# A two-block transformer on one core: attention steps placed by quarters of a unit, weights' high part ahead of chunk steps, first stage reordered

## The chip, the cores and the metric

One NeuronCore of a Trainium2 chip runs the whole program. The metric is device time in microseconds (us) of one execution; lower is better. TensorE is called PE, VectorE DVE, ScalarE ACT, GpSimd POOL, and SP is the queue that issues the weights' transfers.

## The reference

512 tokens of width 1024 go through two blocks of two layers each. A layer of the first block is a gated feed-forward part, a mixer and a second feed-forward part, each behind a root-mean-square norm. The mixer is what the change is about:

```python
h = rms_norm(x, gn[2])
hq, hf, hi, hg, aq, ak, av, gate_a, gate_b = jnp.split(h @ w_in[l], IN_SPLITS, axis=-1)
y_hg = hgrn2_mixer(hq, hf, hi, hg, lb_all[l], hgrn_head_gain[l]) @ w_branch_hgrn[l]
y_at = swa_sink_attention(aq, ak, av, attn_sinks[l]) @ w_branch_attn[l]
mixed = jax.nn.sigmoid(gate_a) * y_hg + jax.nn.sigmoid(gate_b) * y_at
x = x + rms_norm(mixed @ w_out[l], gn[3])
```

`swa_sink_attention` has 8 heads of 64 (2 key heads), blocks of 128 queries that see their own and the previous block of keys, a penalty by distance, and a sink in the softmax. `hgrn2_mixer` is a gated linear recurrence with 4 heads. Weights and activations are float32.

## The kernel before

**Products.** Every weight is scaled and cut into two fp16 parts, as is every activation. ACT makes the high part (`hi`, L1822), DVE the low one (`lo`, L1092), of a slot of 128 x 2048 elements; there are two slots, and SP refills one when its low part is done. A product is three fp16 matmuls (`product`, L466 to L468). A slot of weights is a unit. `hi(s)` waits for the slot's transfer and for the unit that used the slot before, `lo(s)` waits for `hi`, and PE's unit n+2 waits for `lo`, so both run while PE is at unit n+1. A full unit of 256 columns is 48 matmuls of 512 columns.

**The mixer** has 22 units in `MIX_ORDER` (`hf hq hf hi hq aq hg aq hi aq hg aq gate ak gate av` and six times `gate`), then four units of branch products (`branch_part`). Between them PE does small steps, by slots q that `SLOTS` hands to the units. Slots 0 to 22 are the chunk steps of the recurrence: `level_scores` (L664), `diag_scores` (L672), `off_scores` (L687), `head_out` (L695), `head_norm` (L481), `head_scale` (L487); a slot is a chain over the engines. POOL makes exponents (L2211) once PE's scores of a level are done, ACT takes exponentials of them (`decays`, L2000 to L2009) and the root (L1841), DVE makes decayed factors, merges scores and finishes a head (`head_post`, L1381 to L1387). Units of two slots do one of them in the middle, if they are cut in halves, and the other at the end.

**The attention** is cut into 8 items h = 2n + kv (block n, key head kv). An item has three PE steps: `attn_scores` (L722), `attn_transpose` (L732), `attn_out` (L742). In between, DVE subtracts the penalty and finds the maximum (`attn_softmax`, L1397 to L1407), ACT takes exponentials (L2035) and DVE scales them (`attn_probs`, L1419); ACT copies the transposed probabilities (L2040); of the output ACT makes the high part (L2045) and DVE the low part (`attn_low`, L1426), which frees the item's PSUM banks for item h+2. Items 0 and 1 have half the keys. Item kv of block n starts at slot 21 + 3n or 23 + 3n, its steps lie in three slots one after another (`ATTN_SLOT`, `attn_steps`), and slots 23 to 34 hold nothing else. Slots 31 to 34 lie between the first branch products.

Each engine runs its list in order. ACT's and DVE's lists come from loops over units: ACT does unit n's slots, then `hi`, then the evacuation of unit n; DVE does the slots, then waits for the evacuation and makes `lo`.

**The first stage.** PE runs 20 warming matmuls (`warm`, L1027), the bias rows (L1033), 32 warming matmuls, then four transposes of the normed x (`turned`, L503), which fill h by groups g for the first half of the tokens. `first_units` then takes units 0 and 1 in turns: `part(0, g, 0)`, `part(1, g, 0)` for g = 0 to 3. ACT issues the transfers of x blocks 2 and 3 ahead of the square sums of blocks 0 and 1. DVE makes the low weights of unit 0, splits h for groups 0 and 1, makes those of unit 1 (`lo_first`, L1099), splits groups 2 and 3 (L1140), and copies the bias rows.

## Time and profile before

| | us |
|---|---|
| three runs, median | 2728.15 (2725.31 to 2728.27) |
| the profiled execution | 2728.2 |
| its span in the trace | 2726.4 |
| PE busy | 2689.0 |
| DVE busy | 1846.8 |
| ACT busy | 1323.3 |
| POOL busy | 144.2 |

Layer 1's mixer ends with the branch and output products behind 640 us of the trace, layer 2's behind 1658. A busy PE is drawn with modelled ends: a matmul of 512 columns is drawn 0.38 us long while the next one starts 0.216 us after it. An idle time before an instruction is given in brackets with what ended it.

### The profile page before, as it was taken

How to read it: one execution, taken by the hardware profiler on the slowest of the kernel's cores; microseconds unless marked ns; L12 is line 12 of the kernel's file. 1: busy time of each engine (PE TensorE's matmuls, PEld its weight loads, DVE VectorE, ACT ScalarE, POOL GpSimd, SP SyncE). 2: the span in 40 equal slices, each digit the busy share in tenths (PEclk: the TensorE clock that was granted, in tenths of full speed). 3: DMA queues.
4: the chain of work that ended last, by engine and by line, in shares of the span. 5: the costliest groups of instructions: out<-in, count | busy, mean ns of one | idle time of the engine just before them, and what ended most of it. 6: DMA issues, size and time to landing. Idle time of an engine off the chain costs nothing.

```text
span 2726.4 us, 44390 instructions
## 1 busy us (share of the span) xinstructions
PE 2689.0 (99%) x17512; PEld 1730.8 (63%) x17512; DVE 1846.8 (68%) x2793; ACT 1323.3 (49%) x2116; POOL 144.2 (5%) x119
## 2 busy tenths in 40 slices
PE   9999999999999999999999999999999999999998
PEld 6886476644688746885476644688646555465554
DVE  6994376656799628994385656799536776457754
ACT  5663365543566425663365543566424544346442
POOL 1000022100100001000021100100000002000020
PEclk9999999999999999999999999999999999999999
DMA  5443322222333333443312222444333222321312
GB/s 166 110 121 109 116 63 70 89 78 70 109 108 108 123 101 93 122 109 116 109 62 70 90 78 85 124 116 115 120 112 101 78 83 72 111 79 62 109 62 85
DMA packets 317434, 266.18 MB, mean 98 GB/s; under 512 B 8908, under 2 KB 280524, under 8 KB 316656
## 3 DMA queue, kind: packets, MB, share of 16 engines
q1 hardware_dynamic: 314416, 254.57, 30.5%
q10 hardware_dynamic: 2272, 7.58, 1.1%
q0 software_dynamic: 608, 2.11, 0.3%
q8 instruction: 96, 1.57, 0.2%
q14 instruction: 42, 0.34, 0.0%
HBM read 257.40 MB, written 4.21 MB: 96 GB/s over the span
## 4 chain that ended last, share of the span: by engine, by line
PE 93%; DVE 4%; ACT 2%; DVEq 1%; issue 0%; DMA 0%; SPq 0%; ACTq 0%; POOL 0%
PE pu L466 14%; PE pu L467 14%; PE pu L468 14%; PE pm L466 6%; PE pm L468 6%; PE pm L467 6%; PE pu L594 6%; PE pu L592 6%; PE pu L593 6%; PE pm L592 2%; PE pm L594 2%; PE pm L593 2%; PE pm L893 2%; PE pm L664 2%; PE pm L880 1%; DVE w_lo L1092 1%
## 5 line engine op out<-in xcount | busy, mean ns | idle before, releaser
L1092 DVE SCALAR_TENSOR_TENSOR w_lo<-stage,w_hi 128x2048 f16<-128x2048 f32 (+1 forms) x156 | 353.0, 2263 | 393.0 <-ACT w_hi L1822 388.7
L1822 ACT ACTIVATE w_hi<-stage 128x2048 f16<-128x2048 f32 (+1 forms) x147 | 273.3, 1859 | 487.6 <-PE pm L468 376.9
L466 PE MATMUL pu<-h_hi,w_hi 128*128 128x512 f16 x912 | 347.6, 381 | 5.9 <-DVE w_lo L1092 5.9
L467 PE MATMUL pu<-h_lo,w_hi 128*128 128x512 f16 x912 | 347.0, 381 | 0.0
L468 PE MATMUL pu<-h_hi,w_lo 128*128 128x512 f16 x912 | 346.7, 380 | 0.0
L466 PE MATMUL pu<-w_hi,arena 128*128 128x512 f16 x512 | 194.0, 379 | 0.0
L467 PE MATMUL pu<-w_lo,arena 128*128 128x512 f16 x512 | 194.0, 379 | 0.0
L468 PE MATMUL pu<-w_hi,arena 128*128 128x512 f16 x512 | 194.0, 379 | 0.0
L466 PE MATMUL pm<-w_hi,arena 128*128 128x512 f16 x512 | 194.0, 379 | 0.0
L467 PE MATMUL pm<-w_lo,arena 128*128 128x512 f16 x512 | 194.0, 379 | 0.0
L468 PE MATMUL pm<-w_hi,arena 128*128 128x512 f16 x512 | 194.0, 379 | 0.0
L1912 ACT ACTIVATE w_hi<-stage 128x768 f16<-128x768 f32 (+1 forms) x140 | 120.1, 858 | 112.7 <-PE pu L594 112.7
L466 PEld LDWEIGHTS pu<-h_hi,w_hi 128*128 128x128 f16 x912 | 91.1, 100 | 128.8 <-issue 30.6
L468 PEld LDWEIGHTS pu<-h_hi,w_lo 128*128 128x128 f16 x912 | 89.5, 98 | 108.6 <-issue 1.7
L592 PE MATMUL pu<-arena 128*128 128x256 f16 x576 | 157.0, 273 | 0.4 <-ACT arena L1926 0.4
L594 PE MATMUL pu<-h_hi,w_lo 128*128 128x256 f16 x576 | 157.0, 273 | 0.0
L592 PE MATMUL pu<-h_hi,w_hi 128*128 128x256 f16 x576 | 157.0, 273 | 0.0
L593 PE MATMUL pu<-arena 128*128 128x256 f16 x576 | 157.0, 273 | 0.0
L593 PE MATMUL pu<-h_lo,w_hi 128*128 128x256 f16 x576 | 157.0, 273 | 0.0
L594 PE MATMUL pu<-arena 128*128 128x256 f16 x576 | 157.0, 273 | 0.0
L467 PEld LDWEIGHTS pu<-h_lo,w_hi 128*128 128x128 f16 x912 | 89.5, 98 | 95.2 <-issue 3.1
L1234 DVE SCALAR_TENSOR_TENSOR arena<-arena 128x1536 f16<-128x1536 f32 x72 | 126.3, 1754 | 0.0
(332 smaller groups left out, 6227.6 us busy)
## 6 DMA issues: line engine op xcount, KB each, us to landing
stage<-in_w_in_dram SPq DMA_DIRECT2D x136, 512.0 KB, 4.6
stage<-in_w_ffn_gate_dram SPq DMA_DIRECT2D x88, 512.0 KB, 4.0
stage<-in_w_ffn_up_dram SPq DMA_DIRECT2D x88, 512.0 KB, 5.2
stage<-in_w_ffn_down_dram SPq DMA_DIRECT2D x80, 512.0 KB, 4.0
stage<-in_w_out_dram SPq DMA_DIRECT2D x40, 512.0 KB, 4.2
stage<-in_w_in_dram SPq DMA_DIRECT2D x24, 256.0 KB, 3.2
stage<-in_w_ffn_down_dram SPq DMA_DIRECT2D x16, 256.0 KB, 4.2
stage<-in_w_branch_hgrn_dram SPq DMA_DIRECT2D x8, 512.0 KB, 3.5
```

What stands on the lines that cost most here:

```text
L466: nc.tensor.matmul(ps, w1, r_hi, start=first, stop=False)
L467: nc.tensor.matmul(ps, w1, r_lo, start=False, stop=False)
L468: return nc.tensor.matmul(ps, w2, r_hi, start=False, stop=last)
L592: nc.tensor.matmul(ps, w1, r1, start=first and k == 0, stop=False, skip_group_check=not first)
L593: nc.tensor.matmul(ps, w1, r2, start=False, stop=False, skip_group_check=not first)
L594: last = nc.tensor.matmul(ps, w2, r1, start=False, stop=k == 3, skip_group_check=not first)
L664: last = nc.tensor.matmul(pm[i % 2][:, b * P // 2:(b + 1) * P // 2].rearrange("p (n l) -> p n l", l=half), lev[:, 2 * pair + 1, b * P:(b + ...
L893: last = nc.tensor.matmul(ps[:], v_tok[:, b, hd * P:(hd + 1) * P], AT[:, b], start=b == 0, stop=b == NB - 1)
L1092: V.scalar_tensor_tensor(out=w_lo[:, s, 0:n], in0=stage[:, s, 0:n], scalar=WSCALE, in1=w_hi[:, s, 0:n], op0=ALU.mult, op1=ALU.subtract).th ...
L1234: V.scalar_tensor_tensor(out=e_lo[:, 0:1536], in0=sums[:, 4 * s + 1:4 * s + 4].rearrange("p a b -> p (a b)"), scalar=WSCALE, in1=e_hi[:, 0 ...
L1822: A.activation(w_hi[:, s, 0:n], stage[:, s, 0:n], ACT.Copy, scale=WSCALE).then_inc(hi_split, 1)
L1912: return A.activation(w_hi[:, s, first:last], stage[:, s, first:last], ACT.Copy, scale=WSCALE)
```

## The change

- The attention leaves the slots. Each unit from 16 on is done in four quarters, and `ATTN_STEPS` names for each of the three steps the quarter behind which item h has it (a quarter of a unit is 4 of 8 k for one half of the columns; the first four branch products count as quarters 23 to 26). Scores and transpose of an item are four quarters apart from item 2 on, transpose and output one.
- DVE's and ACT's orders from unit 16 on are written out, item by item, in place of the loops.
- In units 3 to 15 ACT makes the high part of the weights (`hi`) behind all but the last slot of the unit, where it did so behind all of them. DVE does the unit's evacuation and `lo` inside the last slot, ahead of `invert_head` and `head_post`.
- First stage: 12 warming matmuls between the second and the third transpose in place of 32 ahead of the first; in the first feed-forward part PE does all four groups of unit 0, then those of unit 1 (`by_unit`); DVE copies the bias rows first and makes unit 1's low weights behind all four splits of h; ACT issues x blocks 2 and 3 behind the high weights of unit 0.

The functions `attn_exp`, `attn_taken`, `attn_high` and `gate` hold what ACT's branches for the attention steps and the gates held. The diff, cut:

```diff
@@ -66,10 +66,12 @@
-SLOTS = consecutive((0, 0, 0, 1, 2, 1, 2, 1, 2, 1, 2, 1, 2, 2, 2, 2, 2, 2, 2, 1, 1, 2) + (0, 2, 0, 2))
-MIX_SLOTS, LAST_SLOTS = SLOTS[:MIX_UNITS], SLOTS[MIX_UNITS:]
+MIX_SLOTS = consecutive((0, 0, 0, 1, 2, 1, 2, 1, 2, 1, 2, 1, 2, 2, 2, 2, 2, 0, 0, 0, 0, 0))
 AHEAD = 4
-ATTN_SLOT = (21, 23)
+ATTN_UNIT = 16
+ATTN_STEPS = ((0, 3, 5, 8, 11, 14, 17, 20), (3, 6, 9, 12, 15, 18, 21, 24), (4, 7, 10, 13, 16, 19, 22, 25))
 MIX2_ORDER = [("aq", 0), ("ak", 0), ("av", 0), ("aq", 1), ("ak", 1), ("ag", 0), ("av", 1), ("ag", 1), ("cu", 0), ("cu", 1),
               ("bq", 0), ("bk", 0), ("bv", 0), ("bg", 0), ("bv", 1), ("bg", 1), ("cg", 0), ("cg", 1)]
@@ -165,14 +167,9 @@
         self.j, self.jper = 0, {}
-def attn_steps(q):
-    found = []
-    for kv in range(2):
-        n, step = divmod(q - ATTN_SLOT[kv], 3)
-        if 0 <= n < NB:
-            found.append((step, 2 * n + kv))
-    return sorted(found)
+def attn_steps(quarter):
+    return [(step, at.index(quarter)) for step, at in sorted(enumerate(ATTN_STEPS), reverse=True) if quarter in at]
...
@@ -517,9 +514,14 @@
                 pe.wait_ge(y_park, t.next("y_park", NB))
                 t.next("evac", 2)
                 pe.wait_ge(split, t.next("split"))
+                if by_unit:
+                    for g in range(4):
+                        pe.wait_ge(h_ready, base + g + 1)
+                        part(0, g, 0)
                 for g in range(4):
-                    pe.wait_ge(h_ready, base + g + 1)
-                    part(0, g, 0)
+                    if not by_unit:
+                        pe.wait_ge(h_ready, base + g + 1)
+                        part(0, g, 0)
                     if g == 0:
                         pe.wait_ge(split, t.next("split"))
                     part(1, g, 0)
...
@@ -762,7 +764,10 @@
                         diag_scores(hd)
                     if step == 4:
                         off_scores(hd)
-                for step, h in attn_steps(q):
+            def attn(quarter):
+                for step, h in attn_steps(quarter):
                     (attn_scores, attn_transpose, attn_out)[step](h)
...
                         col_half(s, 0, P).then_inc(unit_done, 1)
+                    elif n >= ATTN_UNIT:
+                        for i in range(4):
+                            last = col_half(s, i // 2, 256, range(4 * (i % 2), 4 * (i % 2) + 4))
+                            if i == 3:
+                                last.then_inc(unit_done, 1)
+                            if i % 2 and slots:
+                                mixer_slot(slots.pop(0))
+                            attn(4 * (n - ATTN_UNIT) + i - 1)
                     else:
                         col_half(s, 0, 256)
...
                         unit_ready()
                         pe.wait_ge(evac_a, first_a + MIX_ACT - 1 + n)
                         pe.wait_ge(o_ready, t.now("o_ready"))
                     branch_part(n, 0, e)
-                    for q in slots:
-                        mixer_slot(q)
+                    attn(quarter)
                 pe.wait_ge(at_ready, t.next("at_ready", 2))
                 for n in range(4):
...
@@ -1032,14 +1044,16 @@
             for e in range(2):
                 last = nc.tensor.matmul(pm[2 + e][0:A_HEADS, :], rel_tab, rel_hot[:, e * T:(e + 1) * T], start=True, stop=True)
             last.then_inc(rel_done, 1)
-            warm(32)
             pe.wait_ge(id_land, 16)
             pe.wait_ge(xn_ready, 2)
-            for g in range(4):
-                turned(set_b, xn, 0, g)
+            turned(set_b, xn, 0, 0)
+            turned(set_b, xn, 0, 1)
+            warm(12)
+            turned(set_b, xn, 0, 2)
+            turned(set_b, xn, 0, 3)
             for l in range(DEPTH):
                 with t.layers(0, PER1, 1):
-                    ffn(set_a, set_b)
+                    ffn(set_a, set_b, l == 0)
                     mixer()
                     ffn(set_a, set_b)
...
                         levels(hd * 8 + 7)
+                    if unit_work:
+                        unit_work()
                 if step == 1 and 1 <= hd <= HG_HEADS:
                     invert_head()
                 if step == 2 and 1 <= hd <= HG_HEADS:
                     head_post(hd - 1)
-                steps = attn_steps(q)
-                for step, h in steps:
-                    if step == 0:
-                        attn_softmax(h)
-                    if step == 2:
-                        attn_low(h)
-                for step, h in steps:
-                    if step == 0:
-                        attn_probs(h)
+                if unit_work and hd >= HG_HEADS:
+                    unit_work()
             def first_levels():
...
             def mixer():
-                pending = False
                 first_a = t.now("evac_a")
                 lo(1)
-                for n, (kind, part) in enumerate(MIX_ORDER):
+                def unit_work(n):
+                    kind, part = MIX_ORDER[n]
                     s = n % 2
                     banks = set_a[2 * s:2 * s + 2] if n < 2 else pu[2 * s:2 * s + 2]
                     if n == 2:
                         v.drain()
-                    if pending:
-                        v.wait_ge(evac_a, first_a + pending)
-                        pending = 0
+                    if n and evacuated(n, True) > evacuated(n - 1, True):
+                        v.wait_ge(evac_a, first_a + evacuated(n, True))
                     if n == 2:
                         first_levels()
...
                     elif kind == "aq":
                         normed(aq[:, part], banks[0][:], 0.125).then_inc(evac, 1)
-                    else:
-                        pending = evacuated(n + 1, True)
                     if n >= 2:
                         lo(s)
...
@@ -1505,12 +1512,50 @@
                             for b in range(NB):
                                 last = V.tensor_tensor_scan(hG[:, 2 * part + e, b * P:(b + 1) * P], ones[:], tb[:, e, b * P:(b + 1) * P], 0.0, ALU.mult, ALU.add)
                         last.then_inc(g_ready, 1)
-                    for q in MIX_SLOTS[n + 1] if n + 1 < MIX_UNITS else ():
+                for n in range(ATTN_UNIT):
+                    slots = list(MIX_SLOTS[n])
+                    for q in slots[:-1]:
                         mixer_slot(q)
+                    if slots:
+                        mixer_slot(slots[-1], lambda: unit_work(n))
+                    else:
+                        unit_work(n)
+                first_slot, second_slot = MIX_SLOTS[ATTN_UNIT]
+                mixer_slot(first_slot)
+                attn_softmax(0)
+                attn_probs(0)
+                mixer_slot(second_slot)
+                attn_softmax(1)
+                attn_low(0)
+                unit_work(ATTN_UNIT)
+                attn_probs(1)
+                attn_softmax(2)
+                attn_low(1)
+                unit_work(ATTN_UNIT + 1)
+                attn_probs(2)
+                attn_softmax(3)
+                attn_low(2)
+                attn_probs(3)
+                unit_work(ATTN_UNIT + 2)
+                attn_softmax(4)
+                attn_low(3)
+                attn_probs(4)
+                attn_softmax(5)
+                attn_low(4)
+                unit_work(ATTN_UNIT + 3)
+                attn_probs(5)
+                attn_softmax(6)
+                attn_low(5)
+                unit_work(ATTN_UNIT + 4)
+                attn_probs(6)
+                attn_softmax(7)
+                attn_probs(7)
+                unit_work(ATTN_UNIT + 5)
+                attn_low(6)
+                attn_low(7)
                 t.next("o_done")
                 t.next("evac_a", MIX_ACT)
-                for q in sum(LAST_SLOTS, ()):
-                    mixer_slot(q)
                 v.wait_ge(evac_a, first_a + MIX_ACT)
                 for n in range(4):
...
@@ -1781,16 +1826,14 @@
             pre(xn, 0)
             pre(xn, 1)
-            lo_first(0)
-            split_h(set_b, 0, 0, g0)
-            split_h(set_b, 0, 1, g0)
-            lo_first(1)
-            split_h(set_b, 0, 2, g0)
-            split_h(set_b, 0, 3, g0)
             v.wait_ge(rel_done, 1)
             for e in range(2):
                 last = V.tensor_copy(rel_row[:, e * T:(e + 1) * T], pm[2 + e][0:A_HEADS, :])
             last.then_inc(rel_copied, 1)
+            lo_first(0)
+            for g in range(4):
+                split_h(set_b, 0, g, g0)
+            lo_first(1)
             pre(xn, 2)
             pre(xn, 3)
...
+            def attn_exp(h):
...
+            def attn_taken(h):
...
+            def attn_high(h):
...
+            def gate(n):
...
-                for n, (kind, part) in enumerate(MIX_ORDER):
+                for n, (kind, part) in enumerate(MIX_ORDER[:ATTN_UNIT]):
                     banks = set_a[2 * (n % 2):2 * (n % 2) + 2] if n < 2 else pu[2 * (n % 2):2 * (n % 2) + 2]
                     if n == 2:
                         for p in range(AHEAD):
                             decays(p)
+                    for q in MIX_SLOTS[n][:-1]:
+                        mixer_slot(q)
                     if n < 2:
                         s_.wait_ge(unit_done, t.next("unit_done"))
                     else:
                         hi(n % 2)
+                    for q in MIX_SLOTS[n][-1:]:
+                        mixer_slot(q)
                     if kind == "ak":
...
@@ -2073,13 +2135,45 @@
                             last = A.activation(dict(hq=hq, hg=hgs)[kind][:, 2 * part + e], banks[e][:], ACT.Silu, scale=DS)
                         last.then_inc(evac_a, 1)
                     elif kind == "gate":
-                        for e in range(2):
-                            last = A.activation(gates[:, 2 * part + e], banks[e][:], ACT.Tanh, scale=0.5 * DS)
-                        last.then_inc(evac_a, 1)
-                    for q in MIX_SLOTS[n + 1] if n + 1 < MIX_UNITS else ():
-                        mixer_slot(q)
-                for q in sum(LAST_SLOTS, ()):
+                        gate(n)
+                for q in MIX_SLOTS[ATTN_UNIT]:
                     mixer_slot(q)
+                attn_exp(0)
+                hi(0)
+                gate(ATTN_UNIT)
+                attn_taken(0)
+                attn_high(0)
+                attn_exp(1)
+                attn_taken(1)
+                hi(1)
+                attn_high(1)
+                attn_exp(2)
+                gate(ATTN_UNIT + 1)
+                attn_taken(2)
+                attn_exp(3)
+                attn_high(2)
+                hi(0)
+                gate(ATTN_UNIT + 2)
+                attn_taken(3)
+                attn_high(3)
+                attn_exp(4)
+                hi(1)
+                gate(ATTN_UNIT + 3)
+                attn_taken(4)
+                attn_high(4)
+                attn_exp(5)
+                attn_taken(5)
+                hi(0)
+                attn_high(5)
+                attn_exp(6)
+                gate(ATTN_UNIT + 4)
+                attn_taken(6)
+                attn_exp(7)
+                hi(1)
+                attn_high(6)
+                gate(ATTN_UNIT + 5)
+                attn_taken(7)
+                attn_high(7)
...
@@ -2168,9 +2262,10 @@
             root(zero[:, 1:2], ones[:, 0:1], 1.0)
             for b in range(2):
                 s_.wait_ge(x_land[b], 16)
-                A.dma_start(x[:, 2 + b], x_in[:, 2 + b]).then_inc(x_land[2 + b], 16)
                 pre_sums(b)
             hi_first(0)
+            for b in range(2, NB):
+                A.dma_start(x[:, b], x_in[:, b]).then_inc(x_land[b], 16)
             s_.wait_ge(init, 2)
             split_h(set_b, 0, 0, g0)
             split_h(set_b, 0, 1, g0)
```

## Rows read from the trace of the kernel before

**Rows 1.** The page: PE's busy time, and the chain that ended last by engine.
```profile
PE 2689.0 (99%) x17512; PEld 1730.8 (63%) x17512; DVE 1846.8 (68%) x2793; ACT 1323.3 (49%) x2116; POOL 144.2 (5%) x119
...
PE 93%; DVE 4%; ACT 2%; DVEq 1%; issue 0%; DMA 0%; SPq 0%; ACTq 0%; POOL 0%
```

**Rows 2.** PE's waits, whole run: what waited, for whom, us, times, longest.
```profile
PE pm L732 <- DVE arena L1419: 7.2, 6, 1.5
PE pu L466 <- DVE w_lo L1092: 5.9, 4, 1.5
...
PE pm L742 <- ACT arena L2040: 2.3, 2, 1.2
PE pm L695 <- ACT arena L2023: 2.2, 2, 1.1
```

**Rows 3.** Stretches: length, busy by engine, clock, DMA share, GB/s.
```profile
547.12:639.80 92.68, 85.85 (x514) 45.20 (x513) 49.88 (x116) 41.92 (x105) 0.00 (x0) 0.98 0.21 69
1567.02:1658.46 91.44, 84.97 (x514) 44.44 (x513) 49.89 (x116) 41.91 (x105) 0.00 (x0) 1.00 0.21 70
639.80:650.00 10.20, 10.20 (x39) 4.27 (x40) 2.84 (x5) 1.91 (x1) 0.00 (x0) 0.81 0.00 0
1658.46:1668.66 10.20, 10.20 (x48) 4.62 (x48) 4.68 (x5) 1.91 (x1) 0.00 (x0) 1.00 0.00 0
```

**Rows 4.** PE in time order, unit 12: start, length, instruction, idle before.
```profile
483.37 0.59 PE L466 MATMUL pu<-h_hi,w_hi 128*128 128x512 f16 x1 [1.41 <-DVE w_lo L1092]
...
486.92 0.38 PE L466 MATMUL pu<-h_hi,w_hi 128*128 128x512 f16 x1
```

**Rows 5.** ACT in order of time, ahead of that wait.
```profile
474.87 0.44 ACT L2000 ACTIVATE arena<-arena 128x256 f32<-128x256 f32 x1 [6.04 <-POOL arena L2211]
...
478.97 1.90 ACT L1822 ACTIVATE w_hi<-stage 128x2048 f16<-128x2048 f32 x1
```

**Rows 6.** DVE in order of time: one item's softmax, from scores to probabilities.
```profile
560.53 1.42 DVE L1397 SCALAR_TENSOR_TENSOR arena<-cst,pm 128x256 f32<-128x256 f32 x4 [1.19 <-PE pm L722]
...
566.05 0.16 DVE L1414 TENSOR_TENSOR small<-small 128x4 f32<-128x4 f32 x1 [2.27 <-ACT small L2036]
...
566.54 1.14 DVE L1419 TENSOR_SCALAR arena<-arena,small 128x256 f32<-128x256 f32 x4
```

**Rows 7.** Groups by form, 547.12 to 639.80: count, busy us, mean ns, idle.
```profile
L2040 ACT ACTIVATE arena<-pm 128x512 f32<-128x512 f32 x12 | 6.5, 597 | 11.2 <-PE pm L732 11.2
...
L1426 DVE SCALAR_TENSOR_TENSOR arena<-pm,arena 128x256 f16<-128x256 f32 x8 | 3.4, 424 | 9.5 <-ACT arena L2045 8.9
L2045 ACT ACTIVATE arena<-pm 128x256 f16<-128x256 f32 x8 | 3.1, 383 | 23.2 <-PE pm L742 23.2
```

**Rows 8.** ACT and PE in order of time, behind unit 13: chunk step 16.
```profile
510.63 0.44 ACT L2000 ACTIVATE arena<-arena 128x256 f32<-128x256 f32 x1 [0.92 <-POOL arena L2211]
...
513.29 1.28 ACT L1841 ACT_TABLE_LOAD   x1
514.58 0.26 ACT L1841 ACTIVATE r_col<-pm,eps 128x4 f32<-128x4 f32 x1
...
515.38 0.38 PE L487 MATMUL pm<-ident,r_col 128*128 128x128 f32 x2
```

**Rows 9.** DVE and PE in order of time, around unit 10's first matmul.
```profile
455.22 2.28 DVE L1092 SCALAR_TENSOR_TENSOR w_lo<-stage,w_hi 128x2048 f16<-128x2048 f32 x1
...
457.56 0.39 PE L466 MATMUL pu<-h_hi,w_hi 128*128 128x512 f16 x1 [1.53 <-DVE w_lo L1092]
```

**Rows 10.** PE and ACT in order of time, first stage.
```profile
15.47 1.90 PE L503 MATMUL pu<-ident,arena 128*128 128x128 f32 x8 [3.13 <-DVE h_lo L1140]
16.50 1.91 ACT L1832 ACTIVATE arena<-stage 128x2048 f16<-128x2048 f32 x1 [2.74 <-DMA stage<-in_w_ffn_up_dram]
...
20.79 0.28 PE L466 MATMUL pm<-h_hi,arena 128*128 128x256 f16 x1 [1.24 <-DVE arena L1099]
```

**Rows 11.** A stretch of the first stage: PE busy, clock, DMA share, GB/s.
```profile
16.00:20.00 4.00, 3.56 (x19) 0.62 0.92 256
```

52 lines of the change are left out of this document (27 added, 25 removed).

## The prediction

> **What bounds the kernel now.** I read the page's busy shares and its chain first: TensorE (PE) is busy 2689.0 of 2726.4 us and holds 93% of the chain that ended last [rows 1]. So nothing that another engine does counts unless PE waits for it, and all there is to gain is PE's 37.4 us without work plus any stretch in which it ran at half clock. The table of waits names what ended its idle time [rows 2]: the attention's transposes waiting for the softmax on DVE (7.2 us, 6 times), first matmuls of a unit waiting for the low part of their weights (5.9 us, 4 times), the attention's output matmuls waiting for ACT (2.3), a chunk step's head matmul waiting for ACT (2.2). All of it lies in the two mixers of the first block. Two waits more, 3.13 and 1.24 us, stand at the start [rows 10]. Then I cut stretches out. The attention part of layer 1's mixer, from the end of gate unit 16 to the last attention output, takes 92.68 us with PE busy for 85.85; in layer 2 it is 91.44 and 84.97 [rows 3]. The same rows show the clock: the 10.2 us behind it hold 39 matmuls at granted clock 0.81 in layer 1 and 48 at 1.00 in layer 2. In layer 1 part of those 10.2 us ran at 1.2 GHz and not at 2.4, behind three waits that followed each other closely.
>
> **Part 1, attention by quarters.** The work is unchanged; its places change. A quarter of a unit is 12 matmuls, 12 x 0.216 = 2.59 us (0.216 is the usual step from one 512-column matmul's start to the next; the 48 in 10.2 us of layer 2's row give 0.213 [rows 3]). Before, items follow each other at unit ends, and the transpose of item h comes one unit after its scores. For a full item the chain takes, from scores to probabilities, 560.53 to 567.68 = 7.15 us: mask and maximum on DVE 3.3, exponentials on ACT 2.2, scaling 1.63 [rows 6]; a short or half unit doesn't cover it, so PE stood still.
> After, scores(h) and transpose(h) have four quarters and three other attention steps between them, about 13 us. The test is whether the written orders let the chain run in time, so I walked all 26 quarters from 547.12 on with the durations of [rows 6, 7], 1.90 for a high part [rows 5] and 2.29 for a low part [rows 9]. The pattern is the same for every item:
> - From out(h-1) to transpose(h): two quarters and a scores step (about 1.16 us) = 6.3 us. In that time the orders ask for high(h-1) 0.38, then either exponentials 2.2 and scaling 1.63, or low(h-1) 0.42, a whole weights' low part 2.29 and scaling 1.63, with some 0.3 for hand-overs: 4.5 to 5.1. Spare: 1.1 us (items 5 and 2) to 1.8 (item 4).
> - From out(h-2) to scores(h): one quarter, 2.59, against high 0.38 and low 0.42: 1.5 spare.
> - From transpose(h) to out(h): one quarter against two copies of 0.6: 1.3 spare, if ACT is free, which by the orders it is each time.
> - First matmul of units 17 to 21 and of the branches: the low part is there 2.1 to 8 us before it.
> - scores(1) needs head_post(3), which ends as PE comes by; 0 to 0.1 us.
> - Behind out(7) there is now a quarter of a branch, which covers low(7).
> So no wait is left there: layer 1 gives back its idle 6.83 us, layer 2 6.47 [rows 3]; each of the six waits also costs the 0.16 us by which a matmul's drawn 0.38 us exceeds its 0.216 step: 7.8 and 7.4. The clock: within layer 1's stretch the busy time is 0.88 us longer than layer 2's, and behind it 9 matmuls x 0.216 = 1.9 are missing [rows 3]: 2.8. Together **18.0 us**. Bounds: 0, if every wait comes back elsewhere, to 18.0.
>
> **Part 2, high part ahead of the last chunk step (units 3 to 15).** At 483.37 PE waits 1.41 us for a low part, and then takes until 486.92 for nine matmuls, 3.55 instead of 1.94 us [rows 4]. The low part was late because ACT's high part started at 478.97, behind the chunk step's exponentials from 474.87 on, themselves 6.04 us late for GpSimd, and a root [rows 5]. The scores that GpSimd waited for stand behind the unit's end on PE, so the slot was free before that 6 us hole closed: the moved high part runs inside it, and DVE's low part (merges until 475.3, then 2.3) ends near 477.6, before PE's need at 481.95 (483.37 less the wait). Gain 1.46 + 1.61 = 3.1 in layer 1, 3.0 in layer 2: **6.1 us**. The move costs little elsewhere: the exponentials of a step wait for GpSimd, which waits for PE's scores behind the same unit end, about 2 us, and the high part takes 1.90.
> The other pair of these waits (457.5 and its twin, 1.53 each) stays: there DVE's low part at 455.22 starts without a wait for ACT, behind the evacuation of unit 8 and step 8 on DVE itself [rows 9]; the order around it doesn't change. So do the two waits of L695 [rows 2].
> One place gets worse. Unit 13 has both its steps behind it. Before, step 16's exponentials start at 510.63, then a table load and the root, and PE's head_scale goes at 515.38 with 0.3 us to spare [rows 8]. Now high(13) comes between steps 15 and 16: it can start at 509.7 and holds ACT to 511.6, one us past 510.63. Root 515.8, reciprocal 516.1: PE waits about 0.75 us in each layer, **-1.5 us** (between 0 and -3, the latter if the clock also falls as at 483).
> Here a page speaks against the change. The row shows the table load at 513.29 taking 1.28 us and the root starting at 514.58, 1.29 later [rows 8]. The Trainium skill, "ScalarE: Activation LUTs", section "What ACT_TABLE_LOAD costs", charges a switch 2.66 us, load and drain together. By the row this wait is 0.75, by the page's figure it would be 2.1, and the sum 2.7 us smaller; the row decides.
>
> **Part 3, first stage.** PE's transposes 2 and 3 wait until 15.47 for the first low part of h, after lo_first(0) [rows 10]; this chain (weights land, high, low, split) keeps its times, so the removed 20 warm matmuls and the earlier transposes gain nothing; with 12 left, the idle before 15.47 is about as long as it was, 3.1 us, so I leave the clock as it was, low until 19 (granted 0.62 from 16 to 20 [rows 11]). The gain is in the order of units: before, PE needs lo_first(1) right behind the first part and idles 1.24 us until 20.79, since its weights land at 16.5 [rows 10]. After, four parts of unit 0 (1.31 us each) come first, from 17.0 to about 23.2; x blocks 2 and 3 are issued behind hi_first(0), so those weights land some 3 us earlier (two transfers of about 1.5 us less ahead of them), yet lo_first(1) now stands behind all four splits of h and ends at 21.3, 1.9 before it is needed. Gain 1.24 + 0.16 - 0.1 = **1.3 us**, bounds 0 to 2.5 (the low clock's 1.0 too). The moved DMA issues (0.7 us on ACT) and the copies of the bias rows (1.27 us on DVE, now in its hole before lo_first(0)) are hidden; if they weren't, 15.47 would be 0.7 later. x blocks 2 and 3 then land by about 18, as ACT is through with split_h. DVE runs the following h forms without a gap, but all starts from PE's last transposes, so it shifts too.
>
> **Sum.** 18.0 + 6.1 - 1.5 + 1.3 = 23.9 us. PE is the bound from there to the end, so it passes through. The profiled execution took 2728.2 us (span 2726.4), the median of the three runs is 2728.15: 2728.2 - 23.9 = **2704.3 us**.
>
> **Rivals.**
> (A) Waits return at the transposes. The spare is 1.1 to 1.8 us, and one low part more ahead of the scaling (2.29 against about 1.2) gives 1.1 us of wait. For it: the orders are strict, and one late output holds two engines. Against: GpSimd, whose lateness made the hole of [rows 5], has nothing to do there. Six full items x 2 layers x 1.1 = 13: 2717.5.
> (B) Slower than before. The same twelve waits, each followed by a fall of the clock, as the wait of 1.41 us at 483.37 was [rows 4]: 1.1 + 1.9 = 3.0 each, 36 us: 2740. It decides from 23.9 / 12 = 2.0 us per wait on. Against: the wait of 1.53 us until 457.56 left the clock up, its first matmul took 0.39 [rows 9], not 0.59 as at 483.37. The Trainium skill, "TensorE: Matmul & The Clock Gate", section "A second HAM failure mode: psum-queue depth-cycling", tells of just this, small idles between groups of matmuls that make the clock swing; the trace agrees in layer 1 behind 639.80 and not in layer 2 [rows 3]; where such idles come back, that rule gives this rival's time, and layer 2's rows give (A)'s.
> (C) The move of the high part doesn't do what it says: what was late at 483 is then the exponentials for the following step, which now stand behind the high part, and PE waits there. The 6.1 us are gone and 1.5 more are lost, as at unit 13: 23.9 - 7.6 = 16.3, 2711.9.
> (D) More than I count: the waits at 457 and L695 go too (twice 1.53 + 0.16, twice 1.1 + 0.1, 5.8 us): 2698.5.
>
> **How the numbers follow.** Forecast 0.58 (2702 to 2707 by itself), A 0.16, B 0.05, C 0.10, D 0.08, and 0.03 for unforeseen waits that eat all the gain. For 8 in 10 the range takes in D and C, and of A all but its full price (ten of twelve waits are 11 us): 2698 to 2716. Bounds of +-0.2% (5.5 us; about what a measurement of this kernel can tell from no change): faster 0.91, same 0.03, slower 0.06.
>
> **What the profile after would show.** No wait of L732, L742, L722 or of the branch's L466 above 0.2 us in either mixer, and granted clock 1.00 there; one wait for w_lo per layer in place of two; a new wait of head_scale (L487) for the reciprocal, 0.5 to 1 us per layer; idle behind the first transposes as before, none at the first use of unit 1. Wrong would be: waits of transposes for the scaling (A), the same with clock below 1 (B), or level scores waiting for DVE's decayed factors in units 4 to 14 (C).

## The result and the profile after

| | before | after |
|---|---|---|
| median, us | 2727.3 (4 runs, 2725.31 to 2728.27) | 2704.93 (4 runs, 2703.39 to 2705.11) |
| profiled execution | 2728.2 | 2705.11 |
| its span | 2726.4 | 2703.3 |

The ratio of the times is 0.9918, with a 95% interval of 0.99 to 0.9935: 0.8% faster. The forecast was 2704.3.

The page of the changed kernel, PE's busy time and the chain by engine (before: [rows 1]):
```profile
PE 2682.1 (99%) x17492; PEld 1727.2 (64%) x17492; DVE 1837.1 (68%) x2793; ACT 1323.3 (49%) x2116; POOL 139.1 (5%) x119
...
PE 94%; DVE 3%; ACT 1%; DVEq 0%; issue 0%; DMA 0%; POOL 0%; ACTq 0%; SPq 0%
```
PE is the bound as before; it has 21.2 us without work in place of 37.4. Its waits, whole run (before: [rows 2]):
```profile
PE pu L463 <- DVE w_lo L1106: 2.7, 2, 1.5
PE pm L697 <- ACT arena L2066: 2.2, 2, 1.1
PE pu L500 <- DVE h_lo L1154: 2.1, 1, 2.1
PE pu L500 <- DVE arena L1148: 1.5, 1, 1.5
...
PE pm L484 <- DVE r_col L1390: 0.7, 2, 0.3
```
The waits of the attention's transposes (L734 now) and outputs (L744) are gone altogether. One low part per layer is waited for, not two. (In layer 2 a wait of 0.41 us for DVE at L674 now stands 9 us ahead of it, and its own is 1.16 us in place of 1.53: together the same.) The third and fourth lines stand in the first stage, and the last is the new wait of head_scale.

To say where the time went I cut both traces at the same instructions of PE: a head_scale between chunk steps, the next but one, and the first transpose (`turned`) of the feed-forward part behind the mixer. The clock column is the granted clock, 1.00 for 2.4 GHz and 0.50 for 1.2 GHz; matmuls that ran at 1.2 GHz are called slow below. First the kernel before (columns as in [rows 3]; the first two lines are layer 1, then layer 2):
```profile
479.62:546.68 67.06, 64.53 (x433) 41.99 (x432) 43.02 (x83) 34.52 (x59) 9.73 (x8) 0.97 0.30 91
546.68:711.64 164.96, 158.13 (x842) 77.84 (x841) 97.93 (x175) 66.74 (x138) 0.00 (x0) 0.98 0.27 87
1499.43:1566.57 67.14, 64.61 (x433) 41.99 (x432) 43.08 (x83) 34.53 (x59) 9.73 (x8) 0.97 0.30 91
1566.57:1728.40 161.83, 155.35 (x841) 76.62 (x840) 97.67 (x175) 66.68 (x138) 0.00 (x0) 1.00 0.28 88
```
The same stretches of the changed kernel:
```profile
478.90:543.32 64.42, 62.98 (x434) 41.48 (x432) 39.41 (x81) 32.41 (x58) 7.80 (x8) 1.00 0.30 92
543.32:698.20 154.88, 154.88 (x842) 76.39 (x840) 96.42 (x175) 66.37 (x138) 0.00 (x0) 1.00 0.29 92
1485.99:1550.42 64.43, 62.98 (x433) 41.47 (x432) 39.38 (x81) 32.42 (x58) 7.81 (x8) 1.00 0.29 92
1550.42:1705.30 154.88, 154.88 (x841) 76.39 (x840) 96.23 (x175) 66.33 (x138) 0.00 (x0) 1.00 0.29 92
```
The borders give the lead of the changed kernel (how much sooner it reaches the same instruction), and the lengths give what each stretch adds:

| stretch | layer 1 | layer 2 |
|---|---|---|
| lead as the chunk stretch begins | 0.72 | 13.44 |
| chunk stretch | 67.06 - 64.42 = 2.64 | 67.14 - 64.43 = 2.71 |
| attention stretch | 164.96 - 154.88 = 10.08 | 161.83 - 154.88 = 6.95 |
| lead as it ends | 13.44 | 23.10 |

The lead stays 23.1 us to the end, which is the difference of the spans. What counts most is the attention stretch: length and PE's busy time are one number, 154.88, in both layers. PE has no idle time there.

The first stage of the changed kernel, PE's wait ahead of the third transpose and the clock behind it (before: [rows 10, 11]):
```profile
15.60 0.66 PE L500 MATMUL pu<-ident,arena 128*128 128x128 f32 x4 [2.14 <-DVE h_lo L1154]
```
```profile
16.00:20.00 4.00, 3.87 (x21) 2.88 (x20) 2.79 (x6) 3.23 (x8) 0.00 (x0) 0.57 0.96 262
```
The wait of 1.24 us for unit 1's low part is gone, but the granted clock was 0.57 here, below before's 0.62: twelve products ran at 1.2 GHz, three more than before. The lead is 0.7 us.

The wait at head_scale behind unit 13, on ACT and on PE (before: [rows 8]):
```profile
505.72 1.89 ACT L1865 ACTIVATE w_hi<-stage 128x2048 f16<-128x2048 f32 x1
507.52 0.42 ACT L2043 ACTIVATE arena<-arena 128x256 f32<-128x256 f32 x1
...
510.15 1.28 ACT L1884 ACT_TABLE_LOAD   x1
511.44 0.26 ACT L1884 ACTIVATE r_col<-pm,eps 128x4 f32<-128x4 f32 x1
```
```profile
511.97 0.65 PE L484 MATMUL pm<-ident,r_col 128*128 128x128 f32 x4 [0.32 <-DVE r_col L1390]
```
The high part now stands ahead of step 16's exponentials, and they start right as it ends. PE waits 0.32 us; by `hi13_both` below, which takes this wait out, it costs 0.54 us in each layer.

### The profile page after: what moved, and what is told of

Same layout as the page of the kernel before. It is cut to its first block, busy times and chain, and to the rows that moved or that the text cites. A ratio compares the mean times of both kernels' runs of the same rounds, so it can differ in the third digit from the quotient of the medians.

```text
span 2703.3 us, 44352 instructions
## 1 busy us (share of the span) xinstructions
PE 2682.1 (99%) x17492; PEld 1727.2 (64%) x17492; DVE 1837.1 (68%) x2793; ACT 1323.3 (49%) x2116; POOL 139.1 (5%) x119
## 3 DMA queue, kind: packets, MB, share of 16 engines
q8 instruction: 96, 1.57, 0.2%
## 4 chain that ended last, share of the span: by engine, by line
PE 94%; DVE 3%; ACT 1%; DVEq 0%; issue 0%; DMA 0%; POOL 0%; ACTq 0%; SPq 0%
PE pu L463 14%; PE pu L464 14%; PE pu L465 14%; PE pm L465 6%; PE pm L463 6%; PE pm L464 6%; PE pu L595 6%; PE pu L594 6%; PE pu L596 6%; PE pm L594 2%; PE pm L595 2%; PE pm L596 2%; PE pm L905 2%; PE pm L666 2%; PE pm L892 1%; PE pm L697 1%
## 5 line engine op out<-in xcount | busy, mean ns | idle before, releaser
L1239 DVE SCALAR_TENSOR_TENSOR w_lo<-stage,w_hi 128x1536 f16<-128x1536 f32 x72 | 126.0, 1750 | 0.0
```

Of the source, the lines that this page charges most:

```text
L1239: V.scalar_tensor_tensor(out=w_lo[:, s, 512:], in0=stage[:, s, 512:], scalar=WSCALE, in1=w_hi[:, s, 512:], op0=ALU.mult, op1=ALU.subtract) ...
```

## The experiments

Medians of before are those of runs on the same chip in the same session: 2727.13 for the first four kernels, 2725.43 for the next four, 2728.2 for the last four. The theory was that the three parts are worth what the cut traces show, each by itself. The rivals were that they need one another, and that part of the lead is a matter of the clock and not of the change.

**Each part alone.** `start_only` is the kernel before with the first stage of the change:
```
-            warm(32)
...
+            turned(set_b, xn, 0, 0)
+            turned(set_b, xn, 0, 1)
+            warm(12)
...
-                    ffn(set_a, set_b)
+                    ffn(set_a, set_b, l == 0)
```


> The kernel before with the reordered first stage alone (order of the turns, the row of the slopes copied ahead of the first split, the loads of x2 and x3 sent later, unit 0's up products of all four groups ahead of the gate's); nothing is left out. The prediction's term: 1.3 us shorter. Theory 1, from the two traces compared event by event (the changed kernel leads by 0.7 us from its first gate products on): the first stage is worth 0.7 us, and this kernel alone shows the same 0.7 us, because nothing later reaches back to it; its slow stretch of the clock ends some 0.7 us later than in the kernel before. Theory 2, the term was right and the rest was lost later, in the first chunk of the changed kernel: this kernel then leads by 1.3 us at the first gate products and ends 1.3 us sooner.

Measured: 2723.79 us, ratio 0.999 (0.998 to 0.9999). Its trace is 4.9 us shorter than that of before, in two steps, neither of them the one expected. The first stage leads by 2.4 us, not by 0.7, since the clock was up in it:
```profile
16.00:20.00 4.00, 3.88 (x36) 3.36 (x35) 3.16 (x6) 3.71 (x8) 0.00 (x0) 1.00 0.98 265
```
The other 2.7 us come in layer 1's attention, which this kernel has unchanged:
```profile
544.38:706.60 162.22, 155.36 (x841) 76.61 (x840) 97.93 (x175) 66.84 (x138) 0.00 (x0) 1.00 0.28 88
1561.56:1723.43 161.87, 155.36 (x842) 76.66 (x841) 97.67 (x175) 66.79 (x138) 0.00 (x0) 1.00 0.28 88
```
The first line was 164.96 at clock 0.98 in the profiled run of before. So layer 1's slow stretch behind the old attention isn't there each time. Both theories fell: this experiment shows how far such stretches come and go. It may be more than chance: the profiled execution, without the slow stretch, took 2723.36 us, and the slowest of the ten of `start_only` 2724.73, which is less above it than one such stretch costs; the twenty of before lie between 2723.72 and 2729.69. If so, the stretch came in none of the ten, and part of the 3.3 us in the medians is that and not the first stage. What in the first stage would keep the clock up 500 us later isn't known.

`chunk_only` is the kernel before with the weights' high part ahead of the last chunk step:
```
+                    ahead = MIX_SLOTS[n][:-1] if n < 16 else MIX_SLOTS[n]
+                    for q in ahead:
+                        mixer_slot(q)
...
+                    for q in MIX_SLOTS[n][len(ahead):]:
+                        mixer_slot(q)
...
-                    for q in MIX_SLOTS[n + 1] if n + 1 < MIX_UNITS else ():
-                        mixer_slot(q)
```


> The kernel before with the weights' high part ahead of the chunk steps alone (ScalarE's high part and VectorE's unit work put inside the last slot of each of the first 16 units); nothing is left out. Theory 1, terms add up: 3.2 us in the first layer and 3.3 us in the second are gained, less a wait of unit 13 at its head_scale product of 0.3 to 0.8 us a layer: 5.3 to 5.9 us shorter than the kernel before, and the new wait stands in this kernel too. Theory 2, the move shows its worth only beside the new attention schedule, since that one sets where the steps of units 13 to 17 start: then this kernel gains clearly less, under 4 us, with waits of products on the weights' high part still there. The rival of the prediction that the move does not do what it says gave 0 us.

Measured: 2722.44 us, ratio 0.9984 (0.9975 to 0.9994). The chunk stretches are those of the changed kernel (before 67.06 and 67.14), and its attention, the old one, tells of the clock again:
```profile
479.56:543.98 64.42, 62.98 (x434) 41.46 (x433) 39.42 (x81) 32.40 (x58) 7.80 (x8) 1.00 0.30 92
543.98:705.81 161.83, 155.35 (x842) 76.65 (x840) 97.95 (x175) 66.73 (x138) 0.00 (x0) 1.00 0.28 88
1493.61:1558.03 64.42, 62.98 (x434) 41.46 (x433) 39.42 (x81) 32.41 (x58) 7.79 (x8) 1.00 0.30 93
1558.03:1722.65 164.62, 158.15 (x841) 77.56 (x840) 97.76 (x175) 66.69 (x138) 0.00 (x0) 0.98 0.28 87
```
2.64 + 2.72 = 5.4 us, as theory 1 has it, and the new wait of head_scale stands here too (0.33 us in each layer); the part needs no other. This time the slow stretch of the attention stands in layer 2 and not in layer 1.

`attn_only` is the changed kernel with the old first stage and the old chunk order:
```
-                    for q in MIX_SLOTS[n][:-1]:
+                    for q in MIX_SLOTS[n]:
                         mixer_slot(q)
...
-                    for q in MIX_SLOTS[n][-1:]:
-                        mixer_slot(q)
```


> The changed kernel with the order of the first stage and of the chunk steps put back as before, so that the local attention by quarters is all that differs from the kernel before; nothing is left out. Theory 1, terms add up: 10.1 us in the first layer and 6.9 us in the second, 17.0 us shorter than the kernel before. Theory 2, the quarters need the earlier unit work: then waits of attention products on VectorE's or ScalarE's steps show up in the trace which the changed kernel does not have, and the gain is below 15 us. The prediction's own term was 18.0 us.

Measured: 2712.13 us, ratio 0.9944 (0.9927 to 0.996), 15.0 us less than before; its trace is 15.9 us shorter.
```profile
547.77:702.65 154.88, 154.88 (x841) 76.40 (x840) 96.48 (x175) 66.46 (x138) 0.00 (x0) 1.00 0.29 92
1557.60:1712.48 154.88, 154.88 (x842) 76.42 (x841) 96.29 (x175) 66.41 (x138) 0.00 (x0) 1.00 0.29 92
```
Again 154.88, twice, and no wait of an attention step: against the profiled before 10.1 + 6.9 = 17.0 us, theory 1, though the chunk order is the old one. The 15.0 of the median stand at the edge of theory 2, but its waits aren't there; 2.8 of the 17.0 are the slow stretch, which before doesn't have each time. The missing 1.1 us lie in its first stage, 1.0 us behind that of before, which has the same code. The gains below before in the three medians are 3.3, 4.7 and 15.0, together 23.0; the change as a whole has 22.4. That they add up so well is partly luck, as the part of `start_only` shows.

**The wait at head_scale.** `hi13_last` puts ACT's high part of unit 13 behind both steps:
```
-                    for q in MIX_SLOTS[n][:-1]:
+                    ahead = MIX_SLOTS[n] if n == 13 else MIX_SLOTS[n][:-1]
+                    for q in ahead:
```


> The changed kernel with one edit: at unit 13 ScalarE makes the high part of the weights behind both of the unit's steps, as the kernel before did, instead of ahead of the last one; nothing is left out. Theory 1, the wait of the head_scale products at slot 17 (0.3 us in each layer, and 0.5 us lost against the kernel before) is the price of that high part being ahead: the wait goes, and the kernel is 0.3 to 0.5 us a layer shorter, 0.6 to 1.0 us in all. Theory 2, the high part of unit 13 is then late for its own products: the wait moves there, and the time is the same or up to 1 us longer a layer.

Measured: 2717.48 us, ratio 0.9965 (0.9951 to 0.9979), 12.5 us more than the changed kernel, against both theories. PE and then DVE:
```profile
515.35 1.11 PE L484 MATMUL pm<-ident,r_col 128*128 128x128 f32 x4 [3.56 <-DVE r_col L1390]
```
```profile
512.91 2.29 DVE L1106 SCALAR_TENSOR_TENSOR w_lo<-stage,w_hi 128x2048 f16<-128x2048 f32 x1 [3.55 <-ACT w_hi L1865]
515.12 0.17 DVE L1390 RECIPROCAL r_col<-r_col 128x4 f32<-128x4 f32 x1
```
ACT was sooner with the root, as meant. But on DVE the reciprocal stands behind the low part, the low part needs the high part, and that had become the later one. An order that is written out on two engines can't be changed on one. The chunk stretch took 70.74 us in place of 64.42: a wait 3.2 us longer cost 6.3, because the clock was down for the 16 score matmuls and 6 products behind it.

`hi13_both` changes the order on DVE as well:
```
+                    if n == 13:
+                        mixer_slot(slots[-1])
+                        unit_work(n)
+                    elif slots:
```


> The changed kernel with unit 13 in the old order on both engines: ScalarE makes its high part behind both steps, and VectorE does the unit's own work behind the whole of the last step; nothing is left out. The run before this one moved it on ScalarE alone, and TensorE then waited 3.56 us at the head_scale products, because VectorE's copy of the root's result stood behind its low part, and that behind the high part. Theory 1, the changed kernel's 0.32 us wait at the head_scale products (0.54 us lost a layer) comes of the order on both engines: with both put back the wait is gone and the kernel is 0.5 us a layer shorter than the changed one, 1.0 us in all. Theory 2, the low part of unit 13, now some 3 us later, is late for the products that read it: a wait of 0.5 to 2 us on VectorE's low part shows up a layer, and the kernel is longer than the changed one by up to 2 us in all, more if the clock falls behind it.

Measured: 2703.42 us, ratio 0.9918 (0.9901 to 0.9934). The chunk stretches:
```profile
478.19:542.07 63.88, 62.76 (x434) 41.57 (x433) 39.39 (x81) 32.54 (x58) 7.81 (x8) 1.00 0.30 93
1484.75:1548.63 63.88, 62.76 (x433) 41.56 (x432) 39.38 (x81) 32.54 (x58) 7.80 (x8) 1.00 0.30 93
```
64.42 - 63.88 = 0.54 us a layer, the wait is gone and no low part is late. That is theory 1, and the price of moving the high part at unit 13.

**The waits the change left.** `unit8_first`:
```
+                    if n == 8:
+                        unit_work(n)
+                        mixer_slot(slots[-1])
+                    elif slots:
```


> The changed kernel with one edit: at unit 8 VectorE does the unit's own work (evacuation and the weights' low part) ahead of the chunk step instead of inside it; nothing is left out. The changed kernel still waits 1.53 us for the weights' low part at the first product of the next unit in the first layer, about as in the kernel before. Theory 1, what delays that low part is VectorE's queue: it then ends some 1.6 us sooner, the wait is gone, 1.2 to 1.7 us a layer. Theory 2, the chunk step that now stands behind it comes late for TensorE: a wait of 0.5 to 1.5 us moves to the step's products, and the time is the same within 0.5 us a layer. If the low part waits for ScalarE's high part rather than for VectorE, nothing moves at all.

Measured: 2703.04 us, ratio 0.9916 (0.9899 to 0.9932). No wait for a low part is left; the low part starts at 452.14 and PE's product comes at 455.31, unhindered:
```profile
452.14 2.28 DVE L1106 SCALAR_TENSOR_TENSOR w_lo<-stage,w_hi 128x2048 f16<-128x2048 f32 x1
```
```profile
455.31 0.38 PE L463 MATMUL pu<-h_hi,w_hi 128*128 128x512 f16 x1
```
It gains 1.7 us in layer 1 and 1.3 in layer 2 (its lead over the kernel before grows from 0.56 to 2.26 and from 14.98 to 16.30 up to the next head_scale, while the changed kernel's is the same at both), which is the wait of 1.5 and of 1.2 us and the drawn overhang of a matmul. It was DVE's queue, as [rows 9] suggested, and the step put behind it was in time.

`av_split`:
```
+                    if kind == "av":
+                        token_unit(s, P, range(2))
+                        mixer_slot(slots.pop(0))
+                        token_unit(s, P, range(2, NB)).then_inc(unit_done, 1)
```


> The changed kernel with one edit: TensorE does the chunk step of slot 19 in the middle of unit 15, between the second and third token blocks of its products, instead of behind all of them; nothing is left out. The changed kernel waits 1.1 us a layer at the products of that head's output for ScalarE's evacuation. Theory 1, this wait is an unfilled stretch and the unit's other half (24 products, some 1.4 us) fills it: 1.1 us a layer shorter, 2.2 us in all. Theory 2, the inputs of slot 19 are not ready half a unit sooner: the wait moves to the front of the step, and the gain is below 0.5 us a layer.

Measured: 2702.02 us, ratio 0.9914 (0.9898 to 0.9931). The wait of L697 is gone, and the chunk stretches are 64.42 - 63.12 = 1.3 us shorter in each layer:
```profile
478.26:541.38 63.12, 62.79 (x434) 41.42 (x432) 39.42 (x81) 32.53 (x58) 7.80 (x8) 1.00 0.30 94
1484.07:1547.18 63.11, 62.79 (x433) 41.40 (x432) 39.41 (x81) 32.53 (x58) 7.81 (x8) 1.00 0.30 95
```

**The clock of the first stage.** `warm_more`:
```
+            warm(14)
             pe.wait_ge(id_land, 16)
...
-            warm(12)
+            warm(32)
```


> The changed kernel with more filler matmuls in the first stage: 14 ahead of the first turn, and 32 in place of 12 between the second and the third; they write a bank that nobody reads, and nothing is left out. In the changed kernel the clock had risen at 12.96 us, the engine idled from 13.45 to 15.60 us, and from 16.38 to 19.79 us it ran at 1.2 GHz, 4 turns and 12 products at twice their time, 1.7 us; in the kernel with the first stage alone the same stage ran at 2.4 GHz throughout behind an idle of 1.55 us. Theory 1, a shorter idle keeps the clock up: no slow stretch behind the third turn, 1.7 us sooner at the gate's products than in the profiled run of the changed kernel. Theory 2, it is the phase of the stage and not the idle: the slow stretch is there or not there as by chance, and in the timed runs the kernel stands within 0.5 us of the changed one. Theory 3, the clock is still down when the 32 run (0.21 us each, 6.8 us): then the third turn is late by up to 2.3 us.

Measured: 2705.44 us, ratio 0.9922 (0.9906 to 0.9939). The clock was 1.00 from 16 to 20 us and the lead there 2.3 us. But that doesn't show that the idle decides: `start_only` had clock 1.00 behind an idle of 1.55 us, and `late_one` (below), with the first stage of the change and 1.56 us of idle, had 0.65 and a lead of 0.7. Chance, theory 2, fits all of it, though one execution of each can't settle it. The same trace has something that no theory had, in the chunk stretches:
```profile
477.28:544.50 67.22, 66.10 (x434) 43.10 (x433) 39.65 (x81) 32.41 (x58) 7.66 (x8) 0.95 0.29 88
1487.17:1552.71 65.54, 64.42 (x433) 42.34 (x432) 39.50 (x81) 32.41 (x58) 7.74 (x8) 0.97 0.29 91
```
The clock fell there for 12 and for 6 products (the last of each only in part), with no wait between them and those of 455 and 1465. The median is 0.5 us above that of the changed kernel, and the profiled execution, 2707.39, is the slowest of the four.

**How much the attention can bear.** `late_one` and `late_three` make the probabilities of items 2 to 7 late by one and by three additions on DVE:
```
+                if h >= 2:
+                    for _ in range(3):
+                        V.tensor_tensor(ta[:].rearrange("p a b -> p (a b)"), tb[:].rearrange("p a b -> p (a b)"), tb[:].rearrange("p a b -> p (a b)"), ALU.add)
+                        v.drain()
```
The expectations call an item a quarter: the third quarter is item 2, the eighth item 7.

> The changed kernel with one extra VectorE addition (128x1024, about 1.2 us by the rows of like ones) ahead of attn_probs of the third to eighth quarter in both layers; its result is read by nobody, nothing is left out. It makes the normalized probabilities late. In the changed kernel they end 1.67, 3.88, 2.16, 1.68, 1.67 and 3.95 us ahead of the transposes that read them. Theory 1, these spares are real: 1.2 us fits in each, no wait appears, and the time is that of the changed kernel within 0.5 us. Theory 2 (the prediction's rival A in small), the spare is used up further on, at the next softmax, which stands behind the probabilities in VectorE's queue, or at the units' low part: waits appear at the scores, the transposes or the next unit's products, 1 to 5 us a layer.

Measured: 2704.47 us, ratio 0.9919 (0.9906 to 0.9933). One addition took 1.22 us, and both attention stretches are 154.88 us long as before it, with DVE busy 7.3 us more in the first:
```profile
546.11:700.99 154.88, 154.88 (x842) 76.42 (x841) 103.71 (x181) 66.46 (x138) 0.00 (x0) 1.00 0.29 92
1553.87:1708.75 154.88, 154.88 (x841) 76.41 (x840) 103.44 (x181) 66.42 (x138) 0.00 (x0) 1.00 0.29 92
```
The spare of over 1.2 us is real, at every item from item 2 on: theory 1. The median is that of the changed kernel, though two of the five executions, the profiled one among them, took 2708.5 us: its chunk stretches, ahead of the attention, ran slow (last section).

> As the run with one extra addition, with three of them (about 3.5 us) ahead of each attn_probs from the third quarter on; nothing is left out. Theory 1, spares by the trace: waits at the transposes of the third, fifth, sixth and seventh quarter of 1.8, 1.3, 1.8 and 1.8 us, none at the fourth and the eighth: 6.7 us a layer, 13 us in all, and after waits this long the clock falls in some layers, 1.7 to 2.8 us each, as it did in one of two layers of the kernel before. Theory 2, the quarters are a ring, so that each wait also moves what TensorE does next and gives the following quarter its time back: about 3 us a layer. Theory 3, VectorE becomes the bound of the stage: 6 times 3.5 us on top of its work, less its idle time there, 10 us or more a layer.

Measured: 2733.78 us, ratio 1.0019 (1.0008 to 1.0029): slower than the kernel before. The three additions took 3.82 us.
```profile
543.37:714.93 171.56, 161.21 (x841) 78.26 (x840) 118.41 (x193) 66.73 (x138) 0.00 (x0) 0.97 0.26 83
1567.15:1735.81 168.66, 157.97 (x841) 76.83 (x840) 118.15 (x193) 66.69 (x138) 0.00 (x0) 0.99 0.26 85
```
```profile
PE pm L734 <- DVE arena L1437: 18.8, 10, 2.1
```
The stage is 16.7 and 13.8 us longer, nearest to theory 3 by its number, but not by its reason: DVE was busy for only 118 of the 172 us. Theory 1 has the first four waits right in place and nearly in size (2.1, 2.0, 2.1 and 2.1 us by the rows, for a delay of 3.8 and not 3.5), and item 3 waits for nothing. But item 7 waits 0.9 to 1.3 us in spite of its spare of 3.95, and the next products wait 1.1 for their low part: these spares aren't there once DVE is late with all of its queue. PE's idle time is 10.4 us in layer 1 and 10.7 in layer 2; the rest, 6.3 and 3.1 us, is slow matmuls and the drawn ends. The difference of the layers, 2.9 us, is the clock: 17 matmuls of layer 1 ran slow behind the waits, 4 of layer 2.

**A better kernel.** `three_edits` is the changed kernel with the edits of `hi13_both`, `unit8_first` and `av_split`.

> The changed kernel with three of the edits measured singly: unit 13 in the old order on both engines, unit 8's own work ahead of its step on VectorE, and the step of slot 19 in the middle of unit 15 on TensorE; nothing is left out. Theory 1, terms add up: 0.54 and 0.55, 1.70 and 1.62, 1.30 and 1.30 us in the two layers, 7.0 us shorter than the changed kernel at the same state of the clock, 2698 us. Theory 2, with the work of units 8, 13 and 15 closer together on VectorE a wait comes back at slot 17 or at the products of unit 15 or 16: 5 us or less.

Measured: 2699.61 us (2698.44 to 2700.07), ratio 0.9898 (0.9883 to 0.9914). Its chunk stretches:
```profile
476.92:541.17 64.25, 64.25 (x434) 42.21 (x433) 39.52 (x81) 32.65 (x58) 7.93 (x8) 0.97 0.30 92
1482.51:1545.09 62.58, 62.58 (x434) 41.50 (x432) 39.39 (x81) 32.64 (x58) 7.81 (x8) 1.00 0.30 95
```
Layer 2 has 64.43 - 62.58 = 1.85 = 0.54 + 1.3 us, and 1.3 more ahead of it, the same as singly: the terms add up, though the 1.62 us that I had put down for unit 8 in layer 2 was too much. In layer 1 PE is never idle either, but six products ran slow, and 1.67 us are missing.

> The changed kernel itself once more, with no edit and nothing left out: how far its stages differ from one execution to the next, and its median beside the kernel of three edits on the same chip. If the stretches at 1.2 GHz are a matter of chance, its first stage lies between 0.6 and 2.4 us ahead of that of the kernel before as first profiled (0.7 in its first profile), and the chunk steps may have a slow stretch of 1 to 2.3 us without a wait ahead of it, as the kernel with more filler had; its attention stages gain 10.1 and 6.9 us as before, since they held no slow stretch and no wait. If the lead of the first stage is a constant of the program, it is 0.7 us again.

Measured: 2705.02 us (2704.73 to 2705.17), ratio 0.9919 (0.9906 to 0.9933). `three_edits` is 5.4 us below it on the same chip, and the two sets of runs don't overlap. The second trace is the first one over again, with a lead of 0.74 us from the first stage and these stretches of layer 1:
```profile
478.88:543.29 64.41, 62.97 (x433) 41.45 (x432) 39.38 (x81) 32.39 (x58) 7.79 (x8) 1.00 0.30 92
543.29:698.17 154.88, 154.88 (x841) 76.42 (x840) 96.44 (x175) 66.34 (x138) 0.00 (x0) 1.00 0.29 92
```

## Why the prediction was right

The sum was 23.9 us, and the trace has 23.1. The mechanism of each part was right; that the total came so near is partly luck, as the errors of the four terms (-1.0, +0.3, +0.4 and -0.6 us) take each other back, and single executions of before differ by up to 6 us. Term by term:

| term | predicted | measured |
|---|---|---|
| attention by quarters | 10.6 + 7.4 | 10.08 + 6.95 |
| high part ahead | 3.1 + 3.0 | 3.18 + 3.26 |
| head_scale behind unit 13 | -0.75 a layer | -0.54, -0.55 |
| first stage | 1.3 | 0.7 |

- Attention. The walk through 26 quarters gave a spare of 1.1 to 1.8 us; `late_one` used up 1.2 of it without a wait, and `late_three` shows what rival A looks like. Its delay is 3.8 us against the 2.3 of rival A, so its 2.1 us a wait don't gainsay A's 1.1. But the waits came with 3 to 6 us a layer more, for slow matmuls and ends, and that A had at nothing. The mis-sized step is the 0.16 us that I added for each of six waits. The idle time of layer 2's stretch went in full (161.83 - 155.35 = 6.48), but PE's busy time fell by 0.47 us and not by 0.96. A likely reason is that the quarters enter attention steps more often, 22 times in the stretch against 10: in the changed kernel a product at 592.47 is followed by the outputs 0.31 us later, against 0.216 from product to product. This was not tried by itself.
- The clock behind the old attention. I counted 2.8 us for layer 1 from one trace [rows 3]. The mechanism is right, waits and then slow matmuls, yet it struck in 2 of the 6 layers with the old attention that were profiled (before, `start_only`, `chunk_only`), each time for 2.8 to 3.1 us. A fair term was a third of that for each layer, some 1.9 us in all. With it the attention is worth about 16 us on the average of executions, and `attn_only` has 15.0 in its median, with a first stage that was 1.0 us behind in its one profile. Six layers are few, and the ten even executions of `start_only` speak against a plain chance of a third.
- High part ahead. The step was right in its place too: the high part ran from 471.36 in the 6 us hole and the low part ended at 476.77, which with the lead of 0.72 is 477.5 in the time of before, where the forecast said 477.6. The sum had 1.46 us for the wait; the row's 1.41 with the 0.16 of a drawn end is 1.57, and with the 1.61 of the slow matmuls this gives the 3.18 measured. In all 6 layers with the old order the wait of 1.41 to 1.43 us was there and the chunk stretch ran at 0.97, in five of them slow right behind the wait; in 15 of 20 with the new one (`hi13_last` apart) there was neither. So rival C is out. It has one exception: 5 of the 20 (`warm_more`, `late_one`, `three_edits`) had a slow stretch of 1.1 to 2.8 us without that wait.
- head_scale. The mechanism was right, the size 0.2 us a layer too large. In the time of before, which is that of the changed kernel plus its lead of 3.90 us here, the high part started at 509.62 (forecast 509.7) and step 16's exponentials at 511.42: 0.8 us later than their 510.63, and not a full us. The root came 0.76 us later than it would have (514.58 less 3.90 is 510.68; it came at 511.44), and PE's head_scale 0.49 us (515.38 less 3.90 is 511.48; it came at 511.97). So the spare was 0.27 us, as the forecast had it. The row also decides against the page as it did before: load and root start 1.29 us apart. By the 2.66 us that the Trainium skill, "ScalarE: Activation LUTs", section "What ACT_TABLE_LOAD costs", charges for a switch, PE would have waited some 1.7 us here, an estimate; it waited 0.32.
- First stage. The wait of 1.24 us went as predicted, but I had left the clock as it was, low until 19 us; it was low until 19.7, and three more products ran slow. Averaged over the ten traces with the new first stage (0.56 to 2.38; `warm_more` left out) the lead is 1.0 us, and over three with the old one (0, 0.05, -1.0) it is -0.3: the difference is the 1.3 of the forecast. Three are few, and without `attn_only` it would be 1.0. The profile of one execution was the wrong thing to hold it against.
- Rival B. Waits did let the clock fall, but not each time: the Trainium skill, "TensorE: Matmul & The Clock Gate", section "A second HAM failure mode: psum-queue depth-cycling", tells of small idles that make the clock swing, and `late_three` agrees with it in layer 1 (17 slow matmuls) far more than in layer 2 (4 behind as many waits). By that rule alone the chunk stretch of `late_one` would have had no fall; it had 12 slow products at 507 to 512 us, with PE never idle since 457.
- Rival D. The waits at 457 and L695 stayed, as the forecast said. `unit8_first` and `av_split` show that both were a matter of the order on DVE and on PE.

## What to carry to other kernels

Where an order is written out by hand, walk each engine's queue through it once and note the spare at every hand-over; then test the spare with a delay of just that size, which tells at once whether a gain is safe. If a step is moved on one engine, look on each other engine for what stands behind the work that waits for it, and move that as well. Hold a term against a stage cut out of several traces: stages without a slow stretch repeated to 0.02 us here, and those with one differed by up to 3 us.

## What the runs showed of the hardware

The clock was the surprise. PE can drop to 1.2 GHz without having waited just before. In `late_one` its last wait ended at 456.8 us, it was busy without a gap up to 511.9, and yet:
```profile
495.00:507.40 12.40, 12.40 (x72) 9.00 (x71) 7.54 (x13) 6.95 (x15) 3.96 (x4) 0.92 0.28 87
507.40:511.90 4.50, 4.50 (x12) 1.57 (x11) 4.04 (x8) 4.25 (x11) 0.19 (x1) 0.50 0.27 58
```
In other executions of the same order it kept 1.00 there. In layer 2 of `attn_only` eight products ran slow at 1519.4 to 1523.0, some 25 us behind the wait of 1.42 us that ended at 1494.21. The six falls of this kind (two each in `late_one` and `warm_more`, one each in `three_edits` and `attn_only`) have their place in common: each began in one and the same group of score matmuls (L666, 128x64), with 72 products of the chunk stretch behind it. So the place is the program's, and whether the clock falls there differs from one execution to the next; what decides it is open. Such falls go along with the spread of the kernel before, 2723.7 to 2730.0 us over all its runs: of the twenty of the first session, the six with the lowest mean clock (0.996) took 2728.1 to 2729.7 us, the seven with the highest (0.998) 2723.7 to 2726.4. One slow stretch behind the old attention costs 2.8 to 3.1 us, but which stretch was slow in an execution without a profile isn't known.
